# Two transformer blocks on one core: both attentions' calls written out in a new order

## What is computed

```python
def second_block(x, ...):
    for layer in range(DEPTH):
        x = x + 0.5 * swiglu(rmsnorm(x, ffn1_norm[layer]), ...)
        hn = rmsnorm(x, mix_norm[layer])
        y = nsa_mixer(hn, ...) if layer == 0 else diff_mixer(hn, ...)
        x = x + y
        x = x + 0.5 * swiglu(rmsnorm(x, ffn2_norm[layer]), ...)

def dense_diff_attention(q, k, v, slopes, lmbda):   # 8 heads, two softmaxes each
    sc = einsum('bhctd,bhcsd->bhcts', qi, k) * scale - slopes * dist
    p = masked_softmax(sc, dist >= 0)
    a = p[:, :, 0] - lmbda * p[:, :, 1]
    return einsum('bhts,bhsd->bhtd', a, v)
# diff_mixer: q, k normalised before; the result normalised per head, then @ w_out
```

## Time and profile before

| | us |
|---|---|
| median of 3 runs | 1311.84 (1309.94 to 1316.11) |
| the profiled execution | 1310.88 |
| its span, first to last instruction | 1309.2 |
| PE busy | 1255.6 (96%) |
| DVE busy | 887.7 (68%) |
| ACT busy | 641.7 (49%) |
| POOL busy | 170.2 (13%) |

### The profile page before, as it was taken

One profiled execution on the slowest core, in us unless ns is written; L12 is line 12 of the kernel. 1 busy time (PEld: TensorE's weight loads), 2 busy tenths in 40 slices (PEclk: granted clock), 3 DMA queues, 4 the chain that ended last, 5 costly groups with the idle time before them and its releaser, 6 DMA issues.

```text
span 1309.2 us, 19606 instructions
## 1 busy us (share of the span) xinstructions
PE 1255.6 (96%) x7778; PEld 1115.8 (85%) x7778; DVE 887.7 (68%) x927; ACT 641.7 (49%) x820; POOL 170.2 (13%) x217
## 2 busy tenths in 40 slices
PE   3999899899999999999999999999999997999998
PEld 2898799798888989877888888888889996888887
DVE  5769766566666667877766667666667776666665
ACT  2445545444444557654644444444445665544442
POOL 8200100188000120110200001000001120200000
PEclk9999899999999999989999999999999999999999
DMA  9887594365555443313455554655554534355551
GB/s 354 283 290 282 169 320 162 129 207 186 190 190 191 136 129 98 129 65 129 160 191 187 186 187 152 222 193 192 192 192 162 161 130 129 129 193 192 192 192 65
DMA packets 166815, 236.87 MB, mean 181 GB/s; under 512 B 5140, under 2 KB 146592, under 8 KB 164704
## 3 DMA queue, kind: packets, MB, share of 16 engines
q1 hardware_dynamic: 165920, 235.09, 53.6%
q0 software_dynamic: 816, 0.89, 0.3%
q10 hardware_dynamic: 16, 0.00, 0.0%
HBM read 234.92 MB, written 1.05 MB: 180 GB/s over the span
## 4 chain that ended last, share of the span: by engine, by line
PE 76%; DVE 12%; DMA 4%; ACT 4%; POOL 1%; issue 1%; DVEq 0%; ACTq 0%
PE acc L2095 22%; PE acc L2097 12%; PE acc L2131 5%; PE acc L2132 5%; PE acc L2133 5%; DVE wlo L1286 3%; PE acc L2113 2%; PE acc L2115 2%; PE acc L2114 2%; DMA raw<-in_w_in_dram 2%; ACT whi L731 2%; DMA raw<-in_w_ada_dram 2%; DVE region L1293 2%; PE acc L2149 1%; PE acc L2032 1%; PE acc L2033 1%
## 5 line engine op out<-in xcount | busy, mean ns | idle before, releaser
L1286 DVE TENSOR_TENSOR wlo<-raw,whi 128x2048 fp32r<-128x2048 f32 (+1 forms) x199 | 454.0, 2284 | 200.7 <-ACT whi L731 199.8
L731 ACT ACTIVATE whi<-raw 128x2048 fp32r<-128x2048 f32 (+1 forms) x199 | 378.5, 1905 | 183.1 <-PE acc L2133 113.1
L2095 PE MATMUL acc<-hT,whi 128*128 128x512 f32 x1280 | 320.1, 392 | 0.0
L2095 PEld LDWEIGHTS acc<-hT,whi 128*128 128x128 f32 x1280 | 232.4, 189 | 43.2
L2097 PEld LDWEIGHTS acc<-hT,wlo 128*128 128x128 f32 x1280 | 174.6, 190 | 12.5
L2097 PE MATMUL acc<-hT,wlo 128*128 128x256 f32 x1280 | 178.5, 282 | 0.0
L2113 PE MATMUL acc<-whi,hT 128*128 128x256 f32 (+1 forms) x432 | 125.8, 291 | 6.2 <-DVE hT L1360 5.8
L2131 PE MATMUL acc<-whi,sT_hi 128*128 128x512 f32 x320 | 125.0, 391 | 0.0
L2132 PE MATMUL acc<-wlo,sT_hi 128*128 128x512 f32 x320 | 125.0, 390 | 0.0
L2133 PE MATMUL acc<-whi,sT_lo 128*128 128x512 f32 x320 | 124.5, 389 | 0.0
L2115 PE MATMUL acc<-whi,hT 128*128 128x256 f32 (+1 forms) x432 | 122.9, 285 | 0.0
(11 more groups left out here) (309 smaller groups left out, 1937.6 us busy)
## 6 DMA issues: line engine op xcount, KB each, us to landing
raw<-in_ffn_w_in_dram SPq DMA_DIRECT2D x88, 1024.0 KB, 5.1
raw<-in_ffn_w_out_dram SPq DMA_DIRECT2D x44, 1024.0 KB, 5.0
raw<-in_w_ada_dram SPq DMA_DIRECT2D x24, 1024.0 KB, 6.1
raw<-in_w_in_dram SPq DMA_DIRECT2D x24, 1024.0 KB, 6.6
raw<-in_diff_w_in_dram SPq DMA_DIRECT2D x12, 1024.0 KB, 5.3
raw<-in_nsa_w_in_dram SPq DMA_DIRECT2D x10, 1024.0 KB, 5.4
raw<-in_w_out_dram SPq DMA_DIRECT2D x8, 1024.0 KB, 4.9
raw<-in_nsa_cmp_w_dram SPq DMA_DIRECT2D x4, 1024.0 KB, 5.4
```

The costliest lines, as they stand in the source:

```text
L731: nc.scalar.activation(whi[:, w % SPL, 0:n], raw[:, r % RAW, 0:n], ACT.Copy).then_inc(hi_ready, 1)
L1286: nc.vector.tensor_tensor(wlo[:, w % SPL, 0:n], raw[:, r % RAW, 0:n], whi_f[:, w % SPL, 0:n], ALU.subtract).then_inc(raw_done, 1)
L2095: nc.tensor.matmul(o, hi[:, kt, cs], hT[:, :, kt, :], start=kt == 0, stop=False)
```

## The change

On ACT, DVE and PE the loop of the differential attention is unrolled into one list of calls, and the calls of both attentions stand in a new order. On POOL `inverse_o` and `inverse_cmpk` get columns of `ms` of their own, so that they share none with other calls. The functions called are the same, apart from small wrappers (`evict_diff`, `lambda_diff`) around what stood in the loop. Cut to the parts that the prediction speaks of:

```diff
-        ms = sb("ms", [P, 16])
+        ms = sb("ms", [P, 33])
...
             def inverse_o(hp):
...
-                step(nc.gpsimd.tensor_scalar(ms[:, 0:4], stat[:, at], 1.0 / P, EPS, ALU.mult, ALU.add))
-                nc.gpsimd.tensor_tensor(rs[:, at], ms[:, 0:4], power[:, 0:4], ALU.pow).then_inc(ors_ready, 1)
+                m = slice(16 + 4 * hp, 20 + 4 * hp)
+                step(nc.gpsimd.tensor_scalar(ms[:, m], stat[:, at], 1.0 / P, EPS, ALU.mult, ALU.add))
+                nc.gpsimd.tensor_tensor(rs[:, at], ms[:, m], power[:, 0:4], ALU.pow).then_inc(ors_ready, 1)
...
@@ DVE, NSA
             scale_k()
+            stream_to(n0 + 5)
             reduce_q(0)
+            gates_ready()
             scale_q(0)
...
             scale_q(2)
+            combine(5)
             evict_nsa_k(3)
-            combine(5)
...
@@ PE, NSA
             nsa_half(4, 0)
+            nsa_half(4, 1)
             turn_q(0)
+            nsa_half(5, 0)
             nsa_scores(0)
-            nsa_half(4, 1)
...
             turn_k(3)
+            nsa_turn(6)
+            cmp_chunk(0, 0)
             turn_q(2)
...
+            cmp_chunk(1, 1)
+            turn_kcn()
             nsa_turn(10)
+            turn_gelu(1)
...
@@ PE, differential attention (the new list from the last projection chunks on)
+            diff_in(10)
+            turn_o(0)
+            turn_qk(3)
+            diff_turn(2, 0)
+            diff_values(1, 1)
+            diff_scores(3, 0)
+            diff_in(11)
+            diff_scores(3, 1)
+            diff_turn(2, 1)
             diff_out(0, 0, 0)
+            diff_values(2, 0)
+            turn_o(1)
+            diff_turn(3, 0)
             diff_out(0, 0, 1)
+            diff_values(2, 1)
             diff_out(0, 1, 0)
+            diff_values(3, 0)
             diff_out(0, 1, 1)
+            diff_turn(3, 1)
             diff_out(1, 0, 0)
+            diff_values(3, 1)
+            turn_o(2)
             diff_out(1, 0, 1)
             diff_out(1, 1, 0)
             diff_out(1, 1, 1)
             diff_out(2, 0, 0)
+            turn_o(3)
             diff_out(2, 0, 1)
             diff_out(2, 1, 0)
             diff_out(2, 1, 1)
-            turn_o(3)
             diff_out(3, 0, 0)
             diff_out(3, 0, 1)
+            turn_x(ENTRY_FFN[3], 0)
             diff_out(3, 1, 0)
-            turn_x(ENTRY_FFN[3], 0)
             diff_out(3, 1, 1)
```

More of the change, by code:

```diff
@@ L1252, in _ @@
-            copy_probs(2, 0)
-            evict_q(3)
+            split_to(d0 + 0 + LEAD)
+            split_to(d0 + 1 + LEAD)
+            evict_diff(0)
+            evict_diff(1)
+            square_qk(0)
+            split_to(d0 + 2 + LEAD)
+            split_to(d0 + 3 + LEAD)
+            evict_diff(2)
+            evict_diff(3)
+            split_to(d0 + 4 + LEAD)
+            square_qk(1)
+            evict_q(0)
+            evict_diff(4)
+            exp_scores(0, 0)
+            exp_scores(0, 1)
@@ new lines, in _ @@
+            copy_probs(0, 0)
+            evict_diff(5)
+            split_to(d0 + 5 + LEAD)
+            split_to(d0 + 6 + LEAD)
+            split_to(d0 + 7 + LEAD)
+            evict_diff(6)
+            square_qk(2)
+            evict_q(1)
+            evict_diff(7)
+            copy_probs(0, 1)
+            exp_scores(1, 0)
+            split_to(d0 + 8 + LEAD)
+            exp_scores(1, 1)
+            evict_o(0, 0)
+            evict_q(2)
+            evict_o(0, 1)
+            copy_probs(1, 0)
@@ new lines, in _ @@
+            split_to(d0 + 9 + LEAD)
+            evict_diff(8)
+            square_o(0)
+            evict_diff(9)
+            square_qk(3)
+            split_to(d0 + 10 + LEAD)
+            exp_scores(2, 0)
+            copy_probs(1, 1)
+            exp_scores(2, 1)
+            evict_o(1, 0)
+            evict_diff(10)
+            evict_q(3)
+            turned_o_hi(0)
+            copy_probs(2, 0)
+            evict_o(1, 1)
+            square_o(1)
+            exp_scores(3, 0)
+            split_to(d0 + 11 + LEAD)
@@ L1268, in _ @@
+            turned_o_hi(2)
             evict_o(3, 1)
             square_o(3)
+            split_to(d0 + 15)
+            split_to(d0 + 16)
             turned_o_hi(3)
@@ new lines, in _ @@
+            stream_to(d0 + 1 + LEAD)
+            reduce_qk(0)
+            stream_to(d0 + 2 + LEAD)
+            scale_qk(0)
+            lambda_diff()
+            stream_to(d0 + 3 + LEAD)
+            evict_k(0)
+            reduce_qk(1)
+            stream_to(d0 + 4 + LEAD)
+            bias_and_max(0, 0)
+            bias_and_max(0, 1)
+            difference(0, 0)
+            scale_qk(1)
+            stream_to(d0 + 5 + LEAD)
+            stream_to(d0 + 6 + LEAD)
+            evict_k(1)
+            difference(0, 1)
@@ new lines, in _ @@
+            stream_to(d0 + 7 + LEAD)
+            bias_and_max(1, 0)
+            reduce_qk(2)
+            bias_and_max(1, 1)
+            difference(1, 0)
+            scale_qk(2)
+            stream_to(d0 + 8 + LEAD)
+            evict_k(2)
+            stream_to(d0 + 9 + LEAD)
+            difference(1, 1)
+            reduce_o(0)
+            bias_and_max(2, 0)
+            reduce_qk(3)
+            bias_and_max(2, 1)
+            scale_o(0)
+            scale_qk(3)
+            difference(2, 0)
@@ L1980, in _ @@
+            evict_k(3)
+            stream_to(d0 + 10 + LEAD)
+            bias_and_max(3, 0)
+            reduce_o(1)
+            difference(2, 1)
+            difference(3, 0)
+            turned_o_lo(0)
+            scale_o(1)
+            bias_and_max(3, 1)
+            turned_o_lo(1)
+            stream_to(d0 + 11 + LEAD)
+            difference(3, 1)
             reduce_o(2)
             scale_o(2)
+            stream_to(d0 + 14)
+            reduce_o(3)
             turned_o_lo(2)
-            difference(3, 1)
+            scale_o(3)
@@ L1984, in _ @@
             stream_to(d0 + 15)
+            turned_o_lo(3)
             stream_to(d0 + 16)
-            reduce_o(3)
-            scale_o(3)
-            turned_o_lo(3)
             join(OUT_DIFF, ENTRY_FFN[3])
@@ L2788, in diff_out @@
                     ins.then_inc(chunk_used, 1)
[L2790 to L2821 removed]
+            diff_in(0)
@@ new lines, in _ @@
+            diff_in(1)
+            diff_in(2)
+            diff_in(3)
+            turn_qk(0)
+            diff_in(4)
+            diff_scores(0, 0)
+            diff_scores(0, 1)
+            diff_in(5)
+            diff_turn(0, 0)
+            diff_in(6)
+            turn_qk(1)
+            diff_in(7)
+            diff_scores(1, 0)
+            diff_turn(0, 1)
+            diff_scores(1, 1)
+            diff_values(0, 0)
+            diff_in(8)
+            turn_qk(2)
+            diff_values(0, 1)
@@ L2822, in _ @@
+            diff_turn(1, 0)
+            diff_in(9)
+            diff_scores(2, 0)
+            diff_scores(2, 1)
+            diff_values(1, 0)
+            diff_turn(1, 1)
+            diff_in(10)
[7 more added lines that the diff above has]
+            diff_turn(2, 1)
             diff_out(0, 0, 0)
+            diff_values(2, 0)
+            turn_o(1)
```

400 lines of the change are left out of this document (134 added, 266 removed).

## The result

The changed kernel took **1290.8 us** (median of 4 runs, 1289.68 to 1295.03) beside 1311.23 us for the kernel before (4 runs, 1309.94 to 1316.11): a ratio of 0.9843, 95% interval 0.981 to 0.9877. A second measurement (six runs) gave 1292.22 us and 0.9852.

A forecast was written before the change was run, and what follows sets the result against it. PE's waits and lower clock in the two attentions, 24.1 us, were taken as the only time to win. Terms of -7.9 (second attention), -0.4 (first, waits) and -4.7 (first, clock) gave -13.0: 1298.9 us, range 1292 to 1307.

The forecast's parts named there:

- What bounds it, and where time could be won: Whole kernel: time can only be won where PE waits or runs at its lower clock; 24.1 us in both attentions.
- No cost for `ms`, no late load: Both attentions: private columns of `ms` cost nothing, and weight loads cost nothing as long as their 5.3 us fit.
- Second attention, waits: Differential attention, mainly its tail: 6.5 us of PE waiting become 0.3, saving 6.2 us.
- Second attention, clock: Differential attention: with PE dense the drop to the lower clock at 1112.5 us goes, saving 1.7 us.
- First attention, waits: NSA attention: 7.4 us of PE waits at other calls against 7.8 before, -0.4 us; bounds 5 and 9.
- First attention, clock: NSA attention: two short stretches at the lower clock remain, 3.4 us lost against 8.1, saving 4.7 us.
- The sum.: Whole kernel: -7.9 - 0.4 - 4.7 = -13.0 us, giving a median of 1298.9 us; chance 0.55.
- Rival 1: Both attentions: the clock never falls, 16.4 us less, 1295.4 us; chance 0.15.
- Rival 2: Only the second attention gains, the first trades waits and keeps its lower clock: -7.9 us, 1303.9 us; chance 0.17.
- Rivals 3 and 4: Narrow margins in both attentions lose half, 1308.4 us, chance 0.08; DVE and PE take turns in the first, 1324 us, 0.05.
- The range: Whole kernel: 8 in 10 for 1292 to 1307 us, from the forecast's own bounds of 1292.7 and 1306.8.

The follow-up runs named there:

- the last run above: Changed kernel with ACT's old list at the head of the first attention and turn_q(0) back between the halves of chunk 4: 1296.79 us, ratio 0.9883.

## Why the prediction was wrong, point by point

- **What bounds it, and where time could be won**: right in the main. PE's waits and its lower clock gave all but 2.2 us of the gain, and the feed-forward stretch did not move. But that time can "only" be won there was wrong, as the point on the stops says.
- **No cost for `ms`, no late load**: right; the stage with the new columns and the old lists took 180.65 us against 180.62, and no load ends a wait of PE in either stage.
- **Second attention, waits**: 6.2 us were to go, and 6.7 went (7.38 to 0.66). The tail has no wait at `turn_o(3)` or `diff_out(3,0,0)`, the 0.3 us of waiting taken for the projection part did not come, and `turn_x` waits 0.3 us.
- **Second attention, clock**: 1.7 us were to come back, and did. With the old order but a full clock the stage took 123.05 us against 124.72.
- **What a stop costs beyond its idle time**: missing from my sum. 1.5 us in the second attention (the rest fell from 115.6 to 114.1), 0.7 in the first: 2.2 us. The run with one turn late shows 0.20 us for one stop, with five stops gone in the second attention. The 0.7 us of the first hang on the estimate of what the clock took, and no run tried them.
- **First attention, waits**: the step that failed most. I had 1.0 + 1.2 + 0.7 + 1.2 + 3.3 = 7.4 us in place of 7.8, so -0.4 us, with bounds of 5 and 9; measured are 3.1 us outside the joins (the rows for L2487, L2495 and L2384), and 4.6 us less in all (8.65 to 4.06). By its places:
  - `turn_q(0)`, 1.0 expected, none came, and 3.0 us to spare. I had moved PE's and DVE's calls and kept `scale_k` at its old time; in truth it comes about 4 us earlier through ACT's list and POOL (shown by the last run above). By the section "Who interferes with whom" of the Trainium skill's page "SBUF — State Buffer", the engine that issues second waits until the other's instruction is over. The trace agrees for POOL behind a split: 2.17 us in the earlier trace rows, and 4.85 us instead of 2.93 for the key's power. I had used it for `scale_q(0)` alone and not for the key's power ahead of it.
  - `turn_q(2)`, 1.2 expected, none came, with 0.74 us to spare. POOL's instruction ahead of it took 0.20 us instead of the 2.17 of the earlier trace rows, 2.0 us less, of which some 1.6 would have reached `scale_q(2)` (POOL done at 532.2 us instead of 530.2, `scale_q(2)` starting at 530.63); the miss is 1.9. That this is the reason was not tried by itself; the split put there shows POOL at 2.17 us again, but hidden behind `nsa_max(7)`.
  - `cmp_chunk(1,0)`, 0.7 expected, none came: its split ended 0.5 us early (551.86 against 552.40). `turn_gelu(1)`, 1.2 expected, none came: ACT's `gelu(1)` ended 0.3 us early (561.73 against 562.03). These two were not tested; my walk was too late at each by 1.2 to 1.5 us.
  - `nsa_values(12)` to `(14)`, 3.3 expected: 1.32 + 0.35 + 1.09 = 2.8 us came, the two long ones for the reason given (`combine` of the step before), the 0.35 behind ACT's `copy_nsa(13)`.
- **First attention, clock**: -4.7 expected with 3.4 us left, one stretch at 468 and one near `nsa_values(12)`. The first profile has 5.1 us left and the second 3.4, with the stretches at these two places. Right.
- **The sum.** By the second profile of the changed kernel the terms are -6.7 - 1.7 - 1.5 in the second attention and -4.6 - 4.7 - 0.7 in the first, -19.9 us, against -13.0: 4.2 us of the miss are the waits of the first attention, 2.2 the stops, 0.5 the waits of the second. The rest of the 8.1 us is 0.6 from the lower median of the kernel before and 0.6 of scatter.
- **Rival 1** (1295.4 us, clock never low) did not happen: the drops near 468 and 581 stayed. The rule cited with it, from the Trainium skill's page "TensorE: Matmul & The Clock Gate" (section "HAM oscillation — how this bites in real kernels"), is that long unbroken gaps bring the lower clock. The trace disagrees: the drop at 581 stood behind waits of 1.3, 0.4 and 1.1 us, and went when they were filled, and the one at 468 stood behind none. **Rival 2** fell with the run of the first attention alone, 9.7 us faster. **Rivals 3 and 4** did not happen either, though the margin of rival 3 is real: 0.74 us at `turn_q(2)`, and one split in the wrong place turned it into 1.44 us of waiting.
- **The range** was too narrow on the fast side. Its lower end came from 5 us of waits with no clock loss; both the stops and a supplier that comes earlier lay outside the bounds I had drawn.

## What to carry to other kernels

When calls move on one engine, walk all the engines again from the start of the stage, the small ones too: here an order on ACT decided whether DVE's long instruction started ahead of POOL's or behind it, and that moved the keys by almost 4 us. Count the stops of the busiest engine and not only its idle time; the one that was put back cost 0.2 us more than it. And after such a change measure how close each new place is to a wait, since a margin of 0.7 us is invisible in a list of waits.
